# A two-layer decoder trunk with product-key experts: GpSimd issues the first table's rows of the next group ahead of the second table's rows of a group

## The reference, cut to what matters

```
s1, i1 = top_k(s[:, :, 0], 16);  s2, i2 = top_k(s[:, :, 1], 16)      # per token and head, 128 keys a side
top_s, top_c = top_k(s1 + s2 (16 x 16), 16)
idx  = i1[top_c // 16] * 128 + i2[top_c % 16]                        # 16 experts of 16384
gate = softmax(top_s)
act  = gelu(einsum('chkd,cd->chk', u_tbl[idx], xc))                  # first table
coef = gate * act
out += einsum('chk,chkd->cd', coef, v_tbl[idx])                      # second table
```

## Time and profile before

| quantity | before |
|---|---|
| median of 3 runs | 1554.36 us |
| the profiled execution | 1554.89 us, of which the span from first to last instruction is 1553.1 us |
| mean granted TensorE clock | 0.826 |
| busy: TensorE, VectorE, ScalarE, GpSimd | 67%, 67%, 26%, 63% of the span |
| moved from HBM | 605.59 MB, 391 GB/s over the span |
| the share of GpSimd's queue | 536.94 MB, 87.3% of 16 DMA engines' time |

### The profile page before, as it was taken

The page is one execution under the profiler, slowest core; times in us unless marked ns, Lnnn a source line. Parts: engine busy times, 40 slices in busy tenths (PEclk is TensorE's granted clock), DMA queues, the critical chain, the costliest instruction groups (busy, mean ns, idle before and its releaser), DMA issues.

```text
span 1553.1 us, 13591 instructions
## 1 busy us (share of the span) xinstructions
PE 1035.4 (67%) x4216; PEld 471.9 (30%) x4216; DVE 1036.3 (67%) x2716; ACT 397.5 (26%) x920; POOL 974.2 (63%) x1041
## 2 busy tenths in 40 slices
PE   9998877655846767736675688787757774444444
PEld 8984422221213332212221334333212221111111
DVE  3367667775777484837676757377778677767673
ACT  1122132222222323222321232333222332112122
POOL 0067757776766655756666665467757767777772
PEclk9999978887967987878887788988979787766667
DMA  9699999999999999999999999999999999999996
GB/s 330 200 343 391 406 406 409 407 406 403 409 409 406 398 405 402 382 407 405 407 406 404 385 401 402 396 373 409 406 406 409 409 410 409 410 409 409 409 409 243
DMA packets 194636, 607.57 MB, mean 391 GB/s; under 512 B 17596, under 2 KB 44292, under 8 KB 194564
## 3 DMA queue, kind: packets, MB, share of 16 engines
q0 software_dynamic: 147456, 536.94, 87.3%
q1 hardware_dynamic: 46976, 69.73, 12.7%
q10 hardware_dynamic: 132, 0.04, 0.0%
HBM read 605.59 MB, written 1.05 MB: 391 GB/s over the span
## 4 chain that ended last, share of the span: by engine, by line
DMA 35%; PE 21%; POOL 17%; DVE 14%; issue 8%; ACT 5%; DVEq 0%; POOLq 0%; ACTq 0%
DMA rows<-in_peer_u,expert 18%; DMA rows<-in_peer_v,expert_v 16%; POOL rows L682 10%; PE sums L967 8%; DVE rows L1820 7%; POOL rows L675 7%; PE banks L783 4%; PE banks L799 4%; DVE coef L1837 2%; ACT soft_diag L1346 1%; PE banks L792 1%; PE sums L792 1%; DMA wring<-in_attn_w_q 1%; PE banks L775 0%; ACT L1331 0%
## 5 line engine op out<-in xcount | busy, mean ns | idle before, releaser
L967 PE MATMUL sums<-rows,soft_diag 128*64 128x512 f32 x2048 | 583.6, 724 | 446.9 <-ACT soft_diag L1346 446.6
L1820 DVE SCALAR_TENSOR_TENSOR rows<-rows,xn_near 128x1024 f32<-128x1024 f32 x512 | 612.6, 1219 | 253.3 <-DMA rows<-in_peer_u,expert 241.3
L682 POOL DMA_INDIRECT rows<-in_peer_v,expert_v x512 | 489.6, 956 | 295.4 <-PE sums L967 159.0
L675 POOL DMA_INDIRECT rows<-in_peer_u,expert x512 | 481.9, 941 | 258.9 <-issue 126.5
L967 PEld LDWEIGHTS sums<-rows,soft_diag 128*64 128x64 f32 x2048 | 162.7, 164 | 841.9 <-ACT soft_diag L1346 541.1
L1346 ACT ACTIVATE soft_diag<-stacked,coef 128x64 f32<-128x64 f32 x512 | 160.7, 343 | 369.8 <-DMA rows<-in_peer_v,expert_v 296.7
L1338 ACT ACTIVATE gelu<-dots 128x8 f32<-128x8 f32 x64 | 13.3, 208 | 446.1 <-DVE rows L1820 444.2
L799 PE MATMUL banks<-wring,xT 128*128 128x512 f32 x160 | 77.3, 636 | 3.4 <-DMA wring<-in_attn_w_q 3.4
L1837 DVE SCALAR_TENSOR_TENSOR coef<-gelu,gate_inv,gate 64x4 f32<-64x4 f32 x256 | 56.8, 222 | 23.4 <-ACT gelu L1338 19.5
L1885 DVE SCALAR_TENSOR_TENSOR soft_diag<-banks,soft_diag 128x512 f32<-128x512 f32 (+1 forms) x8 | 7.7, 958 | 92.7 <-ACT soft_diag L1367 92.7
L783 PE MATMUL banks<-xT,rows 128*128 128x128 f32 x448 | 51.1, 276 | 1.3 <-issue 0.6
(11 more groups left out here) (230 smaller groups left out, 958.6 us busy)
## 6 DMA issues: line engine op xcount, KB each, us to landing
wring<-in_w_kv SPq DMA_DIRECT2D x14, 1024.0 KB, 16.9
rows<-in_peer_u,expert POOLq DMA_INDIRECT x512, 15.0
rows<-in_peer_v,expert_v POOLq DMA_INDIRECT x512, 14.4
wkept<-in_peer_w_query SPq DMA_DIRECT2D x8, 1024.0 KB, 13.7
rows<-in_conv_w_in SPq DMA_DIRECT2D x7, 1024.0 KB, 11.9
wring<-in_peer_w_query SPq DMA_DIRECT2D x7, 1024.0 KB, 13.1
wring<-in_attn_w_q SPq DMA_DIRECT2D x7, 1024.0 KB, 16.5
wkept<-in_conv_w_out SPq DMA_DIRECT2D x4, 1024.0 KB, 12.5
```

The lines of the kernel that those rows point to most:

```text
L675: nc.gpsimd.indirect_dma_start(u_row[j], None, u_table, bass.IndirectOffsetOnAxis(ap=expert[n % 2][:, k:k + 1], axis=0)).then_inc(u_landed ...
L682: nc.gpsimd.indirect_dma_start(v_row[j], None, v_table, bass.IndirectOffsetOnAxis(ap=expert_v[n % 2][:, k:k + 1], axis=0)).then_inc(v_land ...
L967: last = nc.tensor.matmul(sums[side * HP:(side + 1) * HP, half, :], diag[:, g * GROUP + j, :], v_row[j][:, half * 512:(half + 1) * 512], s ...
L1820: nc.vector.scalar_tensor_tensor(out=u_row[j], in0=u_row[j], scalar=1.0, in1=xn_near[:, :, :].rearrange("p a d -> p (a d)"), op0=ALU.mult, ...
```

## The change

In the kernel after, GpSimd's order is u(0) v(0) u(1) v(1) u(2), then u(3) v(2) u(4) v(3) and so on: the first table's rows of group K go ahead of the second table's rows of group K - 1. At the first group of a stage (K of 16, 32, 48) the old order comes back for one group: v(K-1) and then u(K). `combine`, and the diagonals with it, move one slot later in the orders of TensorE and ScalarE (after group 2). ScalarE makes four diagonals of group K - 1, then the gelu of group K, then the other four (all eight ahead of the gelu where a stage begins). VectorE's coefficients stand behind the search for experts and behind the slot's mixer work. The indices of the second table are kept for three steps, and not for two. No work is added or taken away.

```diff
-        expert_v = [sb(f"expert_v{b}", [P, TOPK], U32) for b in range(2)]
+        expert_v = [sb(f"expert_v{b}", [P, TOPK], U32) for b in range(3)]
...
+        FIRST_LATE = GROUPS
+
+        def second_first(K):
+            return K % SLOTS == 0 or K <= FIRST_LATE
...
+            def first_rows(n, g):
+
+                K = GROUPS * n + g
+                if K == 0:
+                    early_weights_used(0)
+                if g == 0 or K == 1:
+                    pool.wait_ge(expert_ready, 1 + K if K < 2 else n + 2)
                 for j in range(GROUP):
...
+                    if K:
+                        pool.wait_ge(dot_done, GROUP * (K - 1) + j + 1)
+                    gather_u(n, g, j)
+
+            def second_rows(n, g):
...
+                for j in range(GROUP) if K else (6, 7, 0, 1, 2, 3, 4, 5):
                     if j % 2 == 0:
-                        pool.wait_ge(v_used, TWOS * (K - 1) + j // 2 + 1)
+                        if K:
+                            pool.wait_ge(v_used, TWOS * (K - 1) + j // 2 + 1)
...
-            first_group()
-            for K in range(1, GROUPS * STEPS):
-                gather_group(K // GROUPS, K % GROUPS)
+            for K in range(GROUPS * STEPS):
+                if second_first(K):
+                    if K:
+                        second_rows(*divmod(K - 1, GROUPS))
+                    first_rows(*divmod(K, GROUPS))
+                else:
+                    first_rows(*divmod(K, GROUPS))
+                    second_rows(*divmod(K - 1, GROUPS))
+            second_rows(STEPS - 1, GROUPS - 1)
...
+            def combine_in_slot(K):
+
+                if K != FIRST_LATE:
+                    n, g = divmod(K if K < FIRST_LATE else K - 1, GROUPS)
+                    combine(n, n % 2, g)
...
+                K = GROUPS * n + g
+                early = GROUP if K % SLOTS == 0 else GROUP // 2
+                if K > FIRST_LATE:
+                    diagonals(K - 1, range(early))
                 act.wait_ge(dot_done, TOPK * n + ks.stop)
                 nc.scalar.activation(gelu[b][:, ks], dots[b][:, ks], ACT.Gelu).then_inc(gelu_done, 1)
-                act.wait_ge(coef_ready, GROUPS * n + g + 1)
-                for j in range(GROUP):
+                if K > FIRST_LATE:
+                    diagonals(K - 1, range(early, GROUP))
+                if K < FIRST_LATE:
+                    diagonals(K, range(GROUP))
...
-                coefficients(n, b, 0)
                 if scored:
                     wait_read(dve, *scored)
                 if look:
...
                     step(n, b, chunk, n + 1 - NH * layer, layer, look=not (last and b == 1), scored=scored)
+                    coefficients(n, b, 0)
                     second_group(n, b, chunk)
+                    coefficients(n, b, 1)
```

More of the change, by code:

```diff
@@ L690, in first_group @@
                 for j in range(GROUP):
-                    if j % 2 == 0 and j:
+                    if K == 0 and j % 2 == 0 and j:
                         early_weights_used(j)
[L693 to L701, removed]
@@ L972, in combine @@
                     last.then_inc(v_used, 1)
-            def combine_pair(i):
-                for b in range(2):
-                    for g in range(GROUPS):
-                        combine(2 * i + b, b, g)
+            def combine_in_slot(K):
+                if K != FIRST_LATE:
+                    n, g = divmod(K if K < FIRST_LATE else K - 1, GROUPS)
+                    combine(n, n % 2, g)
             def transpose_subkeys(layer, quarters=range(2 * HEADS // 4)):
@@ L1235, in _ @@
                 for t in range(SLOTS):
[L1236 to L1237 removed]
+                    combine_in_slot(SLOTS * (1 + c) + t)
                     mixer_slot(c, t)
[L1239 to L1240 removed]
+            first = SLOTS * (1 + CH)
+            combine_in_slot(first)
             query_pair(1, 2)
[L1242 removed]
+            combine_in_slot(first + 1)
             turn_pair(1, 2)
@@ L1245, in _ @@
             query_pair(1, 3)
-            combine(2 * first + 1, 1, 0)
+            combine_in_slot(first + 2)
             turn_pair(1, 3)
             score_pair(1, 3)
-            combine(2 * first + 1, 1, 1)
-            for i in range(first + 1, STEPS // 2 - 1):
-                combine_pair(i)
-            combine_pair(STEPS // 2 - 1)
+            for K in range(first + 3, GROUPS * STEPS + 1):
+                combine_in_slot(K)
             assert taken[0] == len(fills) and halved[0] == len(halves)
@@ L1622, in _ @@
             weigh_pair(STEPS // 2 - 1, last=True)
+            diagonals(GROUPS * STEPS - 1, range(GROUP))
             nc.scalar.preload_act_table_set("natural_log_exp_and_others")
@@ L1717, in halves_of, with experts_by_halves @@
                         yield slice(i * HP, (i + 1) * HP), slice(k0 + j, k1, 2), slice(j * HP, (j + 1) * HP), slice(k0 + i, k1, 2)
-            def experts_by_halves(b, layer):
+            def experts_by_halves(n, layer):
                 for to, rows, tokens, ks in halves_of(0, TOPK):
-                    last = nc.vector.tensor_scalar(expert_v[b][to, rows], expert_f[tokens, ks], float(layer * EXPERTS), None, ALU.add)
+                    last = nc.vector.tensor_scalar(expert_v[n % 3][to, rows], expert_f[tokens, ks], float(layer * EXPERTS), None, ALU.add)
                 last.then_inc(expert_v_ready, 1)
@@ L1868, in second_group @@
                     dot_group(n, b, 1)
-                coefficients(n, b, 1)
             def expert_pair(i, chunk, layer, last=False):
@@ L1993, in _ @@
             second_group(0, 0, 0)
+            coefficients(0, 0, 1)
             conv_group(1, LATER[3])
@@ L1998, in _ @@
                     add_mixer(1)
+                coefficients(n, n % 2, 0)
                 second_group(n, n % 2, 0, ("ffn0", 1) if n == 2 else None)
+                coefficients(n, n % 2, 1)
             for c in range(CH):
@@ L2015, in _ @@
                     mixer_slot(c, t)
+                    coefficients(n, b, t % GROUPS)
             first = (STEPS - HEADS) // 2
@@ L2020, in _ @@
             norm_stream("final", 0)
+            coefficients(2 * first, 0, 0)
             second_group(2 * first, 0, 1)
+            coefficients(2 * first, 0, 1)
             step(2 * first + 1, 1, 1, HEADS + 2, 1, scored=("scoring", 1, 1))
+            coefficients(2 * first + 1, 1, 0)
             second_group(2 * first + 1, 1, 1)
+            coefficients(2 * first + 1, 1, 1)
             for i in range(first + 1, STEPS // 2 - 1):
```

33 lines of the change are left out of this document (13 added, 20 removed).

## The result

Twelve runs of the changed kernel have a median of 1558.20 us (1555.40 to 1560.28), against 1554.12 us of twelve runs of the kernel before (one of them, of 4021.89 us, is left out of the ratio and the scatter): +4.1 us, a ratio of 1.0025 with a 95% interval from 1.0017 to 1.0033. The profiled execution took 1559.27 us with a span of 1557.5 us, 4.4 us more than before each. The change costs a little; the forecast was 1556.7 us with a range of 1552 to 1564. The 4.1 us lie above the 3.1 us that the prediction called no change, on the side to which it gave 0.41.

The account below looks back on a forecast made before the run. Transfers were taken as the bound, with one DMA engine some 8 us behind the others. Terms of -0.9, +2.9 and +0.3 gave +2.3 us, taking the median from 1554.36 to 1556.7 us, range 1552 to 1564.

Parts of the forecast that it names:

- What bounds the kernel: Whole span: transfers bound it, with one DMA engine some 8 us behind the other fifteen setting every landing and the end.
- rival B: Three bandwidth dips belong to all sixteen DMA engines and are filled, so the kernel gets faster: 1549.6 us, chance 0.10.
- The gain at group 38: Deepest dip, share 0.89: factors start without waiting for gelu and coefficients; gain 0 to 1.4 us, taken as 0.9.
- The back-to-back places at the starts: Groups 16, 32, 48: v(K-1) right behind v(K-2) lands late; losses 0.8, 0.3 and 0.8 us.
- VectorE's place behind a stage start: After each of three starts, u(K+2) waits for a dot behind VectorE's search: 0.1 us each, 0.3 (0 to 1.5) together.
- The end: Last group: v(63) right behind v(62) lands late, a loss of 0.5 to 1.5 us, taken as 1.0.
- C, the shallow queue: After stage starts the reserve refills over more than 200 transfers and GpSimd's waits go through: 1564.7 us, chance 0.19.
- E, a shorter way from issue to landing: Transfers turn round faster than the empty-queue rows say, so the four places cost nothing: 1553.8 us, chance 0.08.
- The cover of the gelu: Each group: gelu's 5.1 us wait for four rows is hidden by 11.5 us to VectorE's next rows; otherwise some 5 us.

Follow-up runs that it names:

- e1: Changed kernel without the return to the old order at groups 16, 32 and 48 (late order from group 3): 1558.58 us, ratio 1.0031 to the kernel before.
- e2: Changed kernel with GpSimd back in the old order from group 48 to the end: 1560.60 us, ratio 1.0041 to the kernel before.
- e12: Changed kernel with rows of u(K) and v(K-1) issued two by two in turns at the three stage starts and the end: 1559.37 us, ratio 1.0036.
- e4: Changed kernel with the stage-start order at every fourth group, twelve added places: 1579.36 us, ratio 1.0160 to the kernel before.
- e8: Changed kernel with the gelu behind all eight factors in every group: 1704.01 us where the kernel before takes 1669.31, ratio 1.0236.

## Why the prediction came out as it did

**What bounds the kernel: held.** The filling of all three old dips, 6.6 us of transfers, made nothing faster that the table shows: the shift is 0.3 us ahead of the first (transfer 280) and 0.7 behind it (424), with the search behind the start between them, 1.5 us ahead of the second (transfer 536) and 2.5 us behind it (616), and 2.5 and 2.8 us around the third (616, 680). That is what one DMA engine that runs behind predicts, and rival B, faster by the dips, is refuted. That it is one engine shows in the kernel before from 1538 to 1543 us, where the share of 0.06 is 0.06 x 16 = 1.0 engine:

```profile
1538.00:1543.00 5.00, 5.00 (x20) 1.53 (x18) 0.00 (x0) 2.23 (x7) 0.00 (x0) 0.69 0.06 26
```

**The gain at group 38: 0 in place of -0.9.** From 304 to 383 GB/s in that window, and yet transfer 616 stands 2.5 us later than before and transfer 656 2.4 us. The gain that was to follow from the step "the lagging engine may have stood still too, because the share is 0.89" did not come; 0 was inside its bounds of 0 to 1.4. A smaller gain came where I had none: by transfer 240 the changed kernel, e1, e2 and e12 are 0.7 to 1.3 us ahead. The paragraph on the sum has what the trace shows of it.

**The back-to-back places at the starts: right in kind and nearly in size.** In the table the changed kernel loses 1.0 us from 240 to 280 (0.8 forecast), 0.9 from 472 to 536 (0.3 forecast, bound 0.9), and at 48 it loses 0.7 by transfer 984 together with the search (0.8 and 0.1). e1 and e12, without the places, lose -0.1 and -0.4 from 240 to 280, and -0.2 and -0.4 from 472 to 536. But e2, up to group 47 the same program, loses only 0.2 and 0.8 in these two stretches, so the price of one place is known no better than 0.2 to 1.0 us. The reason in the text was off: I priced how late the first row lands. It lands on time, at 431.61 + 4.6 = 436.2 us, 1.3 us behind the row ahead of it, and the loss is what the rows behind it take on, 4.6 to 6.4 us by the last row of v(15). The two numbers of the earlier trace rows, 5.1 and 6.1 us, which I took for two bounds of one price, fit this growth.

**VectorE's place behind a stage start: the term of the sum that was mis-sized.** Forecast 0.1 each, measured 1.1 from 280 to 376, and 1.2 from 536 to 680 together with group 38 (e2: 0.6 and 1.3). The 13.4 us from the last dot to the next were exact: 458.78 to 472.14. So was "late by -0.5 to 0.5": u(18) landed 1.24 us after its forerunner. What failed is the step from there to 0.1 us: issue to landing grew by 1.4 us over the rows behind u(18)'s first, although that row was not late. In e1 and e12, where v(K-1) is moved back, the stretch from 280 to 376 costs more, 2.0 and 3.7 us.

**The end: 1.6 in place of 1.0,** just over its bound of 1.5. It is the one place shown alone: e12 takes it away, 1.6 to 0.0 us. In e1 and e4, which keep it, it costs 1.2 and 2.0.

**Sum.** By the table -0.7 in the first stage, +1.0 and +1.1 at 16, +0.9 and +1.2 at 32, +0.7 at 48, +1.6 at the end, and -1.3 between the places, give +4.5 us where +2.3 was forecast and the spans differ by 4.4. The -1.3 are stretches with queued work in which both kernels should run alike; they are of the size in which traces of one program differ.

The landings show one thing in these stretches that neither the forecast nor the table counts. With more than 9 us queued and no weights moving, a row lands 1.28 us behind the one ahead of it, but from transfer 101 on 12 landings of the kernel before come 0.93 to 1.01 us late. Ahead of each of the 12, by 1.5 to 2.4 us, a packet of 8 KB of an instruction queue had started; not every such packet has a late landing. Transfer 844 is one of the 12: it lands at 1311.0. The DMA view from 1309 to 1310 us, and issue to landing of transfers 843 and 844:

```profile
q14 instruction: 1, 0.01, 2.1%
rows<-in_peer_v,expert_v POOLq DMA_INDIRECT x1, 12.3
rows<-in_peer_v,expert_v POOLq DMA_INDIRECT x1, 13.3
```

The changed kernel, which has more than 9 us queued for fewer rows, has 6. By transfer 240 the kernel before has 3, the changed kernel and e2 have 2, e1 and e12 have 1: nearly the order of their gains there. Behind start 48 the changed kernel has lost 2.5 us by transfer 808, not 0.7; the kernel before then loses 0.95 and 0.96 at 844 and 887, where the changed one has no such step. So the places cost more than the sum says, and something gives a part back. Whether that is the emptied queue itself, which lets the slow engine catch up with the rest, or chance was not tried. The forecast of the time was good partly by luck: losses of 6.5 us stood where 3.2 were forecast and the forecast gain of 0.9 did not come, but gains of 2.0 us that I had not forecast made up for about half of that.

**C, the shallow queue: out where the kernel before takes 1554 us.** Behind start 48 a row of v(47) takes 7.0 us, and near 1525 us one takes 15.3: the reserve comes back over some 240 transfers, 8.3/240 = 0.035 us each (0.04 forecast). From 752 to 984 the lag grew by 0.7 us, not 8. e4, with 8.4 us from issue to landing in the median, has 1.8 us for a place and not 4. Beside 1660 and 1669 us I can't exclude C. **E, a shorter way from issue to landing,** is right for the first row (4.4 and 4.6 us) and wrong for those that follow. By the fit of the page "DMA: Bandwidth & Descriptors" of the Trainium skill, section on the anatomy of a DMA on GpSimd's path, an estimate of 3.2 us was given; the shortest traced is 4.0 us (e12, u(18)), so the trace does not agree, and the traced rows decide.

**The cover of the gelu: held in the time** as far as e8 can show it, not in its sign. VectorE's wait for the gelu was to stay under a few us. It rose from 19.5 to 93.8 us in the sum, with 7.5 the longest (6.1 before), and GpSimd's waits for the dots rose from 51.8 to 92.0. Some 5 us for each group would have been about 300 us; the change costs 4.1.

## What to carry to other kernels

Price an emptied queue by how issue to landing grows over the rows behind the gap, not only by how late the first one lands: in the changed kernel 1.4 us behind v(15)'s and u(18)'s first rows, 1.7 behind v(63)'s, 2.5 behind v(47)'s (4.5 us, then 7.0), but nothing behind u(50)'s (5.8 us, then 5.8). When transfers are turned past each other, list every consumer of both, the one that needs the older group's result once a stage too (here an addition that waited 11.4 us): a move that helps one empties the queue for the other. And measure such a change more than once, with the kernel before beside it: +4 us beside 1554 us was +45 us beside 1660 us.

## What the hardware showed that I had not expected

- The kernel before took 1669 and 1660 us in two sessions, 7% over the 1554 us of the others, and the record gives the chip of 1660 us and one of 1554 us the same number. Beside the 1660 us the change costs 2.75%, not 0.25%.
- In the changed kernel a 512 KB indirect transfer in an emptied queue took 4.4 to 5.8 us from issue to landing (4.0 in e12), and the eight right behind it 5.8 to 7.0 us in the median, though GpSimd issues them only every 1.24 us.
- With a full queue, 12 landings of the kernel before and 6 of the changed one came 0.9 to 1.0 us late, each 1.3 to 2.4 us behind an instruction packet of 8 KB.
- The same program up to group 47 stood 2.6 us apart in two traces at transfer 752. The changed kernel, whose queue GpSimd's waits run down at seven places, scatters over 4.9 us, and the kernel before over 2.1 us; whether the one comes from the other was not tried.
